# Expert outputs of three quads of four: a scatter by matmul, or indirect DMAs that add rows into sums in DRAM

## The chip, the cores and the metric

The kernel runs on one core of a Trainium2 chip. The metric is the device time of one execution in microseconds (us), as the median of several runs. Everything is float32.

## The reference, cut to what is computed

Two blocks follow each other. The first (two layers of attention, a state-space mixer and cross attention) is untouched by the change. The second has two layers of its own; each ends in a mixture of experts in which the experts choose their tokens:

```python
def _expert_choice_ffn(h, w_router, w_gate, w_up, w_down):
    cap = EC_CAPACITY_FACTOR * t // N_EXPERTS          # 64 of 512 tokens; 32 of 256 context tokens
    aff = softmax(h @ w_router)                        # tokens x 16 experts
    vals, idx = lax.top_k(aff.transpose(0, 2, 1), cap) # every expert picks cap tokens
    xg = h[idx]                                        # 16 x cap x 1024
    hid = silu(xg @ w_gate[e]) * (xg @ w_up[e])        # 1024 -> 512
    out = (hid @ w_down[e]) * vals[..., None]          # 512 -> 1024
    return zeros((t, d)).at[idx.reshape(-1)].add(out.reshape(-1, d))
```

Layer 0 does this for the 512 tokens of the sequence and, apart from them, for 256 context tokens; layer 1 (the last) for the 512 tokens alone. The result, times a modulation vector, is added to `x`.

## The kernel before

One Python program writes each engine's instruction list by hand; engines meet at semaphores. Activations lie feature-major in SBUF: `x` and `h` hold 8 tiles of 128 features by 512 tokens (and 256 context tokens). Matrices are not kept: all weights come from DRAM in the order of their use as one stream of units of 512 KB (128 partitions by 1024 floats). SyncE (SP) issues them (L350) into slots: a ring of 8 (`ring`), and in the expert phase also up to 6 tiles of `y_sb` and, in layer 1, 2 of `work` and 4 of `h_sb`. A slot is refilled when TensorE has turned to the next unit (`w_turn`); the planner `place_units` (L167) lays down which unit goes where. The slots in `y_sb` drop out as the quads' outputs come to need them, so for the last quad of layer 0 there are 10 slots and then 8, for that of layer 1 16 and then 14.

The second block's expert phase (`experts`, L683 for TensorE, L1061 for ScalarE, L1460 for VectorE, L1537 on for GpSimd):

- The router's logits give `aff`; `choose` (L1412) finds the 64 (32) best tokens of each expert and each token's rank among them. The normed tokens are turned token-major, and GpSimd stores them to the DRAM tensor `tokens` (L1560).
- The 16 experts go in four quads. For quad q, `one_hots` (L1442) makes matrices of tokens by slots: 4 blocks of 128 tokens by 4 experts x 64 slots, and for the context 2 blocks by 4 x 32 slots. `slot_tokens` (L734) multiplies them with the column of token numbers; VectorE casts the result to `slot_tok` (L1466), and GpSimd gathers the chosen rows with two indirect DMAs of 128 rows of 4 KB (three with the context; L1567). TensorE turns the rows (`turn_rows`, L745), after a wait for all gathers of the quad.
- Passes over the weights follow in this order: gate 0, then for each quad q: up q, gate q+1, down q (two halves). A pass of 16 units has two matmuls of 64 slots by 512 columns per unit, which run side by side in pairs, and in layer 0 two of 32 context slots, side by side in fours.
- `weigh` (L1451) multiplies the one-hots with the experts' `aff`; `transpose_one_hots` (L758) turns them, 8 transposes (10 with the context), and ScalarE copies them out (`spread_out`, L1102) to `spread`: slots by 512 tokens. The expert outputs stay slot-major in `out_e` (8 tiles of 128 slots by 1024) and `out_c` (4 such tiles, layer 0).
- The scatter is a matmul: for each of 8 feature tiles, `out_e` times `spread`. In layer 0 all of it stands at the end (L866 to L873): per feature tile 8 matmuls of 512 columns and 4 of 256. In layer 1 `scatter(q)` (L768) has two matmuls of 512 columns per feature tile for one quad; the steps of quads 0 to 2 are laid between the weight rounds of the next quad's passes (L805), those of quad 3 at the end. VectorE adds each result, times the modulation, to `x` (L1207 in layer 0, L1480 in layer 1), and in layer 1 SP stores the result (L354).

The helper `mm` is L1595: all matmuls but the transposes carry that line. A float32 matmul is two MATMUL records in the trace, a transpose one.

Of the kernel before, what the change touches and what calls it, by code (L numbers as in the profile page):

```python
# [12 lines left out]
P = 128  # L13
# [21 lines left out]
N_CONST = C_TOKEN + ALL // P  # L35
# [16 lines left out]
def build(nc, names, out):  # L52
# [4 lines left out]
    with ctx:  # L57
# [22 lines left out]
        slot_tok = ctx.enter_context(nc.sbuf_tensor("slot_tok", [P, 4], mybir.dt.uint32))  # L80
# [22 lines left out]
        rows_in = sem("rows_in")  # L103
# [13 lines left out]
        weighted_ready = sem("weighted_ready")  # L117
        quarters_ready = sem("quarters_ready")
        one_hot_read = sem("one_hot_read")
# [412 lines left out]
        def rows_until(both, q):  # L532

            return 3 * q if both else 3 * N_QUADS + 2 * q

# [22 lines left out]
        def slot_groups(both):  # L558
# [3 lines left out]
        spread = ([prob[:, n * T:(n + 1) * T] for n in range(3)] + [flat(10496 + n * T, T) for n in range(3)]  # L562
                  + [flat(n * T, T) for n in range(2)])
        spread_c = [levels_sb[:, n * CTX:(n + 1) * CTX] for n in range(3)] + [flat(2 * T, CTX)]

        def pe_second(pe, me, claim, freed, all_read, mm, weights, project, project_tokens, quarter_squares, add_quarters, attention, unit):
# [116 lines left out]
            def experts(both):  # L683
# [50 lines left out]
                def slot_tokens():  # L734
# [3 lines left out]
                    for n in range(2 + both):  # L738
                        for j in range(4 if n < 2 else 2):
                            of = one_hot[:, j, n * P:(n + 1) * P] if n < 2 else one_hot_c[:, j, :]  # L740
                            ins = mm(banks[6][:, n:n + 1], of, cst(C_TOKEN + j + (0 if n < 2 else 4), 1), j == 0,
                                     j == (3 if n < 2 else 1))
                    ins.then_inc(full_for_dve, 1)

                def turn_rows():  # L745

                    at["rows"] = at.get("rows", 0) + 1
                    pe.wait_ge(rows_in, 16 * rows_until(both, at["rows"]))
                    for n in range(2 * (2 + both)):
                        b = 6 + n % 2  # L750
                        claim(b, "act")
# [6 lines left out]
                def transpose_one_hots():  # L758

                    pe.wait_ge(weighted_ready, me.nth(weighted_ready))  # L760
# [6 lines left out]

                def scatter(q, written):  # L768

                    for f in range(KT):  # L770
                        b = 2 + 3 * (f % 2)
                        if f == 0:
                            pe.wait_ge(freed_by_act, written)
                        claim(b, "dve")
                        for m in (2 * q, 2 * q + 1):
                            ins = mm(banks[b][:, :], out_e[:, m, f * P:(f + 1) * P], spread[m], m == 2 * q, m == 2 * q + 1)
                        ins.then_inc(full_for_dve, 1)
                        yield

                def expert_pass(what, operand, rounds, reader, between=None):  # L780
# [3 lines left out]
                    for r in range(rounds):  # L784
# [20 lines left out]
                        next(at["scatter"], None)  # L805
# [24 lines left out]
                at = {"scatter": iter(())}  # L830
# [3 lines left out]
                expert_pass(("gate", 0), expert_input(0), 4, "act", lambda r: transpose_one_hots() if r == 2 else None)  # L834
                for q in range(N_QUADS):
# [23 lines left out]
                    if not both:  # L859
                        at["scatter"] = scatter(q, freed["act"])  # L860
                if not both:
                    for _ in at["scatter"]:
                        pass
                    return
                all_read("act")
                for f in range(KT):  # L866
                    fs = slice(f * P, (f + 1) * P)
                    for s, (o, sp_, n) in enumerate(((out_e, spread, 8), (out_c, spread_c, 4))):
                        b = 2 * (f % 2) + s
                        claim(b, "dve")  # L870
                        for m in range(n):
                            ins = mm(banks[b][:, 0:(T, CTX)[s]], o[:, m, fs], sp_[m], m == 0, m == n - 1)
# [74 lines left out]
        def act_second(act, me, A, bank_full, evacuate, squares, quarters, deviations, logs, attention):  # L947
# [113 lines left out]
            def experts(both):  # L1061
# [40 lines left out]
                def spread_out(q):  # L1102
                    for n in range(2):
                        evacuate(spread[2 * q + n], banks[6 + n][:, :])
                    if both:
                        evacuate(spread_c[q], banks[6][:, 0:CTX])
                    me.notify(one_hot_read)
# [8 lines left out]
                spread_out(0)  # L1116
# [1415 lines left out]
```

## Time and profile before

| | us |
|---|---|
| median of 3 runs | 3738.31 |
| lowest, highest | 3735.09, 3741.30 |
| the profiled execution's own time | 3735.97 |
| its span (first to last instruction) | 3734.2 |
| TensorE busy in the span | 3488.9 (93%) |
| mean granted TensorE clock | 0.968 |

The expert phase of layer 0 takes the span from about 2440 to 2849 us, that of layer 1 from about 3435 to the end. A span row gives busy time per engine, but a TensorE that is 93% busy over the whole says little on one stage: the stretches and the chain have to be asked stage by stage. A DMA share of 1.0 or more means that all 16 DMA engines always had a packet.

### The profile page before, as it was taken

How to read it: one execution, taken by the hardware profiler on the slowest of the kernel's cores; microseconds unless marked ns; L12 is line 12 of the kernel's file. 1: busy time of each engine (PE TensorE's matmuls, PEld its weight loads, DVE VectorE, ACT ScalarE, POOL GpSimd, SP SyncE). 2: the span in 40 equal slices, each digit the busy share in tenths (PEclk: the TensorE clock that was granted, in tenths of full speed). 3: DMA queues.
4: the chain of work that ended last, by engine and by line, in shares of the span. 5: the costliest groups of instructions: out<-in, count | busy, mean ns of one | idle time of the engine just before them, and what ended most of it. 6: DMA issues, size and time to landing. Idle time of an engine off the chain costs nothing.

```text
span 3734.2 us, 44667 instructions
## 1 busy us (share of the span) xinstructions
PE 3488.9 (93%) x18694; PEld 1959.9 (52%) x18694; DVE 1182.8 (32%) x2505; ACT 911.1 (24%) x1715; POOL 167.8 (4%) x192
## 2 busy tenths in 40 slices
PE   8999999999999989998999988979999999887899
PEld 4455454754465454754755766533334656663333
DVE  2322551022322451022343487120002334673011
ACT  1344130111344130113233321121112224211110
POOL 0000000000000000000000242010000000320000
PEclk9999999999999999999999999989999999799899
DMA  4111172312111172312101001169862110013897
GB/s 149 62 52 46 51 294 77 115 46 67 57 52 45 57 286 75 118 43 92 40 23 45 1 2 41 45 236 355 337 220 92 40 40 29 1 41 141 318 409 314
DMA packets 117414, 425.24 MB, mean 114 GB/s; under 512 B 12768, under 2 KB 14944, under 8 KB 116832
## 3 DMA queue, kind: packets, MB, share of 16 engines
q1 hardware_dynamic: 112896, 406.66, 29.6%
q0 software_dynamic: 4320, 15.73, 1.1%
q8 instruction: 150, 2.46, 0.3%
q14 instruction: 48, 0.39, 0.0%
HBM read 415.00 MB, written 7.34 MB: 113 GB/s over the span
## 4 chain that ended last, share of the span: by engine, by line
PE 85%; DVE 8%; DMA 3%; ACT 2%; issue 2%; POOL 0%; DVEq 0%; SPq 0%; ACTq 0%; POOLq 0%
PE bank L1595 82%; DMA ring<-in_stream 2%; PE bank L1710 1%; PE bank L754 1%; DMA work<-tokens,slot_tok 1%; DMA h_sb<-in_stream 0%; DVE work L1363 0%; DVE h_sb L2270 0%; ACT work L1957 0%; DVE work L2113 0%; DVE work L2115 0%; DVE levels L1363 0%; DVE work L1433 0%; DMA work<-in_stream 0%; DVE small L1432 0%
## 5 line engine op out<-in xcount | busy, mean ns | idle before, releaser
L1595 PE MATMUL bank<-h_sb,ring 128*128 128x512 f32 (+2 forms) x3200 | 1249.4, 547 | 25.5 <-ACT h_sb L972 8.2
L1595 PEld LDWEIGHTS bank<-h_sb,ring 128*128 128x128 f32 (+1 forms) x3200 | 592.5, 190 | 570.2 <-issue 529.7
L1595 PE MATMUL bank<-y_sb,ring 128*128 128x512 f32 (+1 forms) x1152 | 474.1, 573 | 9.7 <-DVEq L205 9.7
L1595 PEld LDWEIGHTS bank<-y_sb,ring 128*128 128x128 f32 x1152 | 219.1, 191 | 259.8 <-issue 245.1
L1917 ACT ACTIVATE work<-bank 128x512 f32<-128x512 f32 (+1 forms) x262 | 133.0, 519 | 797.1 <-PE bank L1595 645.3
L1595 PE MATMUL bank<-work 128*64 128x128 f32 (+7 forms) x2016 | 291.8, 346 | 26.6 <-DVE small L2120 12.2
L1595 PE MATMUL bank<-ring,h_sb 128*128 128x128 f32 (+2 forms) x2144 | 284.8, 311 | 1.4 <-ACT work L1087 0.7
L1595 PEld LDWEIGHTS bank<-ring,h_sb 128*128 128x128 f32 (+2 forms) x2144 | 232.2, 185 | 42.3 <-issue 39.2
L1595 PEld LDWEIGHTS bank<-work 64*128 64x128 f32 (+2 forms) x2016 | 183.6, 170 | 116.2 <-issue 78.8
L1595 PE MATMUL bank<-ring,work 128*64 128x512 f32 (+1 forms) x800 | 210.0, 596 | 0.7 <-DMA ring<-in_stream 0.6
L1595 PE MATMUL bank<-y_sb,work 128*64 128x128 f32 (+2 forms) x920 | 169.2, 430 | 1.4 <-DMA ring<-in_stream 0.7
L1595 PE MATMUL bank<-work,y_sb 128*128 128x512 f32 (+1 forms) x496 | 138.1, 437 | 14.0 <-DVE ring L1335 3.6
L1928 ACT ACTIVATE h_sb<-x_sb 128x1024 f32<-128x1024 f32 (+1 forms) x56 | 48.0, 896 | 407.0 <-DVEq L205 400.8
L1917 ACT ACTIVATE y_sb<-bank 128x512 f32<-128x512 f32 (+1 forms) x163 | 86.8, 555 | 185.0 <-PE bank L1595 172.9
L2125 DVE TENSOR_REDUCE small<-bank 128x1 f32<-128x256 f32 (+3 forms) x96 | 41.7, 466 | 261.5 <-PE bank L1595 261.3
L1548 POOL MEMSET work<- 128x1024 f32 x4 | 3.7, 949 | 2548.4 <-DVEq L205 2548.4
L1595 PEld LDWEIGHTS bank<-ring,work 128*64 128x64 f32 (+1 forms) x800 | 57.4, 129 | 97.4 <-issue 97.3
L1595 PEld LDWEIGHTS bank<-work,y_sb 128*128 128x128 f32 (+1 forms) x496 | 59.5, 170 | 86.4 <-issue 65.2
L1957 ACT ACTIVATE work<-work,small 128x256 f32<-128x256 f32 (+3 forms) x124 | 73.1, 590 | 128.5 <-DVEq L205 128.5
L1595 PE MATMUL bank<-ring 64*128 64x128 f32 x840 | 85.9, 321 | 19.4 <-DVE work L1363 15.9
L1710 PEld LDWEIGHTS bank<-const,work 128*128 128x128 f32 x576 | 69.5, 141 | 57.0 <-issue 40.4
L1595 PEld LDWEIGHTS bank<-y_sb,work 128*64 128x64 f32 (+1 forms) x920 | 61.5, 132 | 69.3 <-issue 64.5
(293 smaller groups left out, 3575.0 us busy)
## 6 DMA issues: line engine op xcount, KB each, us to landing
ring<-in_stream SPq DMA_DIRECT2D x578, 512.0 KB, 4.6
y_sb<-in_stream SPq DMA_DIRECT2D x110, 512.0 KB
h_sb<-in_stream SPq DMA_DIRECT2D x40, 512.0 KB, 14.8
work<-in_stream SPq DMA_DIRECT2D x20, 512.0 KB, 15.3
work<-in_bias SPq DMA_DIRECT2D x2, 2688.0 KB, 9.4
tokens<-work POOLq DMA_DIRECT2D x10, 512.0 KB, 4.5
x_sb<-in_xT SPq DMA_DIRECT2D x4, 512.0 KB, 6.4
out<-x_sb SPq DMA_DIRECT2D x8, 256.0 KB, 2.0
```

Of the source, the lines that this page charges most:

```text
L754: ins = nc.tensor.transpose(banks[b][:, k * P:(k + 1) * P], picked[:, n // 2, ks], ident)
L1548: ins = V.memset(level_sums[d][n], 0.0)
L1595: return nc.tensor.matmul(o, a, b, start=first, stop=last, skip_group_check=True)
L1710: ins = nc.tensor.transpose(banks[b][:, j * P:(j + 1) * P], scores_in(i - 1, s)[:, kb * P:(kb + 1) * P], ident)
L1917: me.link(A(o, i, func, **kw), freed_by_act, wait=False)
L1928: me.link(A(dst[:, k:k + 2, :], src[:, k:k + 2, :], ACT.Square), squares_ready, wait=False)
L1957: me.link(A(at, banks[s][:, 0:u["nk"]] if raw else at, ACT.Exp, bias=nmax[:, j:j + 1], scale=1.0 if raw else -1.0, accum_out=rsum[:, j:j + ...
L2125: me.link(V.reduce_max(m, banks[s][:, 0:nk], AX.X, negate=True), max_ready, wait=False)
```

## The change

1. In both layers the outputs of quads 0 to 2 no longer go through a matmul. GpSimd adds each group of 128 slot rows (512 KB) by an indirect DMA with `compute_op=add` into `sums[l]` in DRAM, at the rows of their tokens (`put_tok`). Two experts of one group may pick the same token, so the two halves of a group add into different copies of the sums (two copies for the tokens, four for the context), and GpSimd waits between DMAs that touch the same copy. That makes 9 such DMAs in layer 0 and 6 in layer 1.
2. After quad 2 GpSimd reads the sums back into `h_tok`: copy 0 plainly, each other copy with an accumulating DMA behind it. Layer 0: six DMAs in four steps (2 x 2 MB and 4 x 1 MB); layer 1: two of 2 MB, one after the other.
3. At the end of each layer TensorE waits for the sums, and per feature tile has quad 3's two matmuls of 512 columns (and one of 256 for the context) and turns the sums by matmuls with the identity into the same bank: 4 of 128 columns (and 2 for the context).
4. `scatter`, `weigh` and their waits go; only quad 3's one-hots are transposed. The slot's weight goes into the product of gate and up (`slot_val`); it comes out of `slot_tokens`, whose moving operand grows from one column to five.
5. The gathers get a semaphore for each group, and `turn_rows` waits for one group at a time.
6. At the start GpSimd fills `sums` with zeros: 24 DMAs of 512 KB after TensorE's twelfth unit. ScalarE waits for them ahead of the first block's second attention.

```diff
                 def slot_tokens():
...
-                            ins = mm(banks[6][:, n:n + 1], of, cst(C_TOKEN + j + (0 if n < 2 else 4), 1), j == 0,
+                            ins = mm(banks[6][:, 5 * n:5 * n + 5], of, token_val[:, j + (0 if n < 2 else 4), :], j == 0,
                                      j == (3 if n < 2 else 1))
                 def turn_rows():
...
-                    pe.wait_ge(rows_in, 16 * rows_until(both, at["rows"]))
                     for n in range(2 * (2 + both)):
                         b = 6 + n % 2
+                        if n % 2 == 0:
+                            pe.wait_ge(rows_in[n // 2], 16 * (at["rows"] + (0 if both or n == 4 else N_QUADS)))
...
-                expert_pass(("gate", 0), expert_input(0), 4, "act", lambda r: transpose_one_hots() if r == 2 else None)
+                expert_pass(("gate", 0), expert_input(0), 4, "act")
...
-                        if r == 2:
+                        if r == 2 and q + 2 == N_QUADS:
                             transpose_one_hots()
...
-                    if not both:
-                        at["scatter"] = scatter(q, freed["act"])
-                if not both:
-                    for _ in at["scatter"]:
-                        pass
-                    return
                 all_read("act")
+                pe.wait_ge(sums_in, 16 * sum(steps_of_sums(n) for n in range(DEPTH - both)))
                 for f in range(KT):
                     fs = slice(f * P, (f + 1) * P)
-                    for s, (o, sp_, n) in enumerate(((out_e, spread, 8), (out_c, spread_c, 4))):
+                    for s in range(1 + both):
                         b = 2 * (f % 2) + s
                         claim(b, "dve")
-                        for m in range(n):
-                            ins = mm(banks[b][:, 0:(T, CTX)[s]], o[:, m, fs], sp_[m], m == 0, m == n - 1)
+                        if s:
+                            mm(banks[b][:, 0:CTX], out_c[:, N_QUADS - 1, fs], spread_c, True, False)
+                        else:
+                            for m in range(2):
+                                mm(banks[b][:, :], out_e[:, 2 * N_QUADS - 2 + m, fs], spread[m], m == 0, False)
+                        for j in range(2 if s else 4):
+                            ins = mm(banks[b][:, j * P:(j + 1) * P], sums_tok[:, 4 * s + j, fs], ident, False,
+                                     j == (1 if s else 3))
                         ins.then_inc(full_for_dve, 1)
```

VectorE, per quad (`chosen_tokens` replaces the cast, `weigh` goes):

```diff
+                me.link(V.tensor_copy(as_rows(slot_tok[:, cols]), found[:, :, 0:1]))
+                me.notify(slots_ready)
+                me.link(V.tensor_tensor(as_rows(put_tok[:, cols]), found[:, :, 0:1], as_rows(cst(C_PUT, n)), ALU.add))
+                for e in range(QUAD):
+                    rows, g = slice(CAP * (e % 2), CAP * (e % 2) + CAP), e // 2
+                    me.link(V.tensor_copy(slot_val[rows, 3 * q + g:3 * q + g + 1], found[rows, g, 1 + e:2 + e]))
...
-                        me.link(V.tensor_tensor(hidden[m], hidden[m], banks[first_bank["up", q] + m][:, :], ALU.mult),
+                        me.link(V.scalar_tensor_tensor(out=hidden[m], in0=hidden[m], scalar=slot_val[:, 3 * q + m:3 * q + m + 1],
+                                                       in1=banks[first_bank["up", q] + m][:, :], op0=ALU.mult, op1=ALU.mult),
                                 freed_by_dve)
```

GpSimd (`rows_scaled` comes from ScalarE when both halves of down q have been copied out):

```diff
+            pool.wait_ge(w_turn, 12)
+            for l in range(DEPTH):
+                for n in range(sums[l].shape[0] // P):
+                    V.dma_start(sums[l][n * P:(n + 1) * P, :], zeros).then_inc(zeros_stored, 16)
...
+                def add_rows(q, n):
+                    o = out_c[:, q, :] if n == 2 else out_e[:, 2 * q + n, :]
+                    V.indirect_dma_start(sums[l], bass.IndirectOffsetOnAxis(put_tok[:, 3 * q + n:3 * q + n + 1], 0), o, None,
+                                         compute_op=ALU.add).then_inc(rows_added, 16)
...
+                for q in range(N_QUADS - 1):
+                    pool.wait_ge(rows_scaled, (N_QUADS - 1) * l + q + 1)
+                    add_rows(q, 0)
+                    if both:
+                        add_rows(q, 2)
+                    if q + 2 < N_QUADS:
+                        fetch_rows(q + 2)
+                    rows_there()
+                    add_rows(q, 1)
+                    if q + 2 < N_QUADS:
+                        rows_there()
+                pool.wait_ge(gather_read, N_QUADS * (l + 1))
+                if both:
+                    read_sums(True, 0)
+                    rows_there()
+                    sums_there()
+                    read_sums(False, 0)
+                    read_sums(True, 1)
+                    sums_there()
+                    read_sums(False, 1)
+                    read_sums(True, 2)
+                    sums_there()
+                    read_sums(True, 3)
+                else:
+                    rows_there()
+                    read_sums(False, 0)
+                    sums_there()
+                    read_sums(False, 1)
+                sums_there()
```

`read_sums(of_ctx, copy)` is one DMA, with `accum_op=add` where copy is not 0. `rows_there()` and `sums_there()` wait for all issued so far.

## Rows read from the trace of the kernel before

**Rows 1.** The page: span, busy time, DMA share (tenths) in 40 slices of the span.

```profile
span 3734.2 us, 44667 instructions
...
PE 3488.9 (93%) x18694; PEld 1959.9 (52%) x18694; DVE 1182.8 (32%) x2505; ACT 911.1 (24%) x1715; POOL 167.8 (4%) x192
...
DMA  4111172312111172312101001169862110013897
```

**Rows 2.** Stretches of chosen length: window, length, busy (instructions) per engine, PEclk, DMA share, GB/s.

```profile
2479.70:2727.00 247.30, 243.93 (x1484) 81.23 (x1472) 16.30 (x24) 39.68 (x75) 8.42 (x9) 1.00 0.90 343
2727.00:2779.00 52.00, 47.39 (x270) 13.52 (x268) 2.06 (x3) 5.82 (x10) 0.00 (x0) 0.97 0.74 271
2779.00:2849.00 70.00, 69.01 (x192) 36.40 (x192) 9.94 (x17) 1.45 (x3) 0.00 (x0) 1.00 0.00 0
3474.70:3707.30 232.60, 226.64 (x986) 82.85 (x984) 29.84 (x39) 29.62 (x51) 5.61 (x6) 1.00 1.02 404
3707.30:3734.20 26.90, 23.58 (x68) 9.07 (x64) 7.51 (x10) 1.19 (x2) 0.00 (x0) 1.00 0.22 84
```

**Rows 3.** Stretches of 20 and 2 us, layer 1's experts, around the weights' last landing.

```profile
3490.00:3510.00 20.00, 19.15 (x102) 8.25 (x103) 1.93 (x4) 2.48 (x5) 1.87 (x2) 1.00 1.03 409
...
3534.00:3536.00 2.00, 1.38 (x8) 0.50 (x8) 0.00 (x0) 0.00 (x0) 0.00 (x0) 1.00 1.05 416
3706.00:3708.00 2.00, 2.00 (x11) 0.77 (x12) 0.75 (x1) 0.00 (x0) 0.00 (x0) 1.00 0.67 262
```

**Rows 4.** The chain that ended last, 2700 to 2860: start, us, what.

```profile
2726.91 6.50 DMA ring<-in_stream
...
2759.12 6.52 DMA ring<-in_stream
...
2779.09 69.03 PE bank L1595 x192
```

**Rows 5.** Timeline in the final scatter of layer 0: start, us, engine, line, operation.

```profile
2839.35 7.03 PE L1595 MATMUL bank<-work,y_sb 128*128 128x512 f32 x16
...
2846.22 1.46 PE L1595 MATMUL bank<-levels,h_sb 128*128 128x256 f32 x6
```

**Rows 6.** Groups by shape over the whole span: busy us, mean ns.

```profile
L1595 PE MATMUL bank<-ring,h_sb 128*128 128x128 f32 x1920 | 220.3, 276 | 0.0
```

**Rows 7.** The chain in layer 0: last gather landing; one-hots turned and copied.

```profile
2467.82 5.12 DMA work<-tokens,slot_tok
...
2548.36 0.60 PE bank L765 x4
...
2548.99 0.61 ACT work L1917
...
2549.64 0.44 PE bank L765 x2
```

**Rows 8.** DMA issues of the page: queue, count, KB each, us to landing.

```profile
tokens<-work POOLq DMA_DIRECT2D x10, 512.0 KB, 4.5
```

**Rows 9.** The chain in layer 1: the gathers of quads 0 and 1 landing.

```profile
3463.16 5.02 DMA work<-tokens,slot_tok
...
3493.27 9.24 DMA work<-tokens,slot_tok
```

**Rows 10.** Stretches of 20 us in which the zeros will be stored, and a cold one.

```profile
100.00:120.00 20.00, 20.00 (x63) 9.04 (x62) 5.29 (x22) 10.71 (x29) 0.00 (x0) 1.00 0.24 79
...
2460.00:2480.00 20.00, 10.03 (x56) 7.96 (x58) 1.81 (x3) 3.70 (x8) 3.27 (x3) 0.59 0.24 79
```

**Rows 11.** Timeline of the last 20 us.

```profile
3715.16 15.72 PE L1595 MATMUL bank<-work,y_sb 128*128 128x512 f32 x36
...
3719.81 12.28 SPq L354 DMA_DIRECT2D out<-x_sb  x8
...
3730.92 0.75 DVE L1480 SCALAR_TENSOR_TENSOR x_sb<-bank,modv_sb,x_sb 128x512 f32<-128x512 f32 x1 [0.97 <-PE bank L1595]
```

More of the change, by code:

```diff
@@ L79, in build @@
         acc_o = sb("acc_o", ALL)
-        slot_tok = ctx.enter_context(nc.sbuf_tensor("slot_tok", [P, 4], mybir.dt.uint32))
+        slot_tok = ctx.enter_context(nc.sbuf_tensor("slot_tok", [P, 12], mybir.dt.uint32))
+        put_tok = ctx.enter_context(nc.sbuf_tensor("put_tok", [P, 12], mybir.dt.uint32))
+        slot_val = ctx.enter_context(nc.sbuf_tensor("slot_val", [P, 12], f32))
+        sums = [nc.dram_tensor(f"sums{l}", (2 * SEQ + (4 * CTX if l < DEPTH - 1 else 0), D_MODEL), f32).ap()
+                for l in range(DEPTH)]
         tokens = nc.dram_tensor("tokens", (ALL, D_MODEL), f32).ap()
@@ L102, in build @@
         slots_ready = sem("slots_ready")
-        rows_in = sem("rows_in")
+        rows_in = [sem(f"rows_in{n}") for n in range(3)]
         w_turn = sem("w_turn")
@@ L560, in slot_groups, with steps_of_sums @@
             return ([(2, CAP_CTX, range(4))] if both else []) + [(0, CAP, (0, 1)), (1, CAP, (2, 3))]
-        spread = ([prob[:, n * T:(n + 1) * T] for n in range(3)] + [flat(10496 + n * T, T) for n in range(3)]
-                  + [flat(n * T, T) for n in range(2)])
-        spread_c = [levels_sb[:, n * CTX:(n + 1) * CTX] for n in range(3)] + [flat(2 * T, CTX)]
+        spread = [prob[:, n * T:(n + 1) * T] for n in range(2)]
+        spread_c = levels_sb[:, 0:CTX]
+        token_val = small[:, 220:250].rearrange("p (j n) -> p j n", j=6)
+        sums_tok = h_tok
+        ZERO_TILES = sum(v.shape[0] // P for v in sums)
+        def steps_of_sums(l):
+            return 6 if need_ctx(l) else 2
         def pe_second(pe, me, claim, freed, all_read, mm, weights, project, project_tokens, quarter_squares, add_quarters, attention, unit):
@@ L1486, in experts @@
-                earlier = iter(())
                 for q in range(N_QUADS):
                     if q + 1 < N_QUADS:
-                        chosen_tokens()
-                    for _ in range(3):
-                        next(earlier, None)
+                        chosen_tokens(q + 1, both)
+                    if q + 2 < N_QUADS:
+                        one_hots(q + 2, both)
                     for m, _, _ in slot_groups(both):
@@ L1561, in _, with fetch_rows @@
                 pool.wait_ge(tokens_stored, 16 * (6 * l + n_tok))
-                for q in range(N_QUADS):
+                both, at = need_ctx(l), {"added": (N_QUADS - 1) * 3 * l, "in": steps_of_sums(0) * l}
+                def fetch_rows(q):
                     pool.wait_ge(slots_ready, N_QUADS * l + q + 1)
@@ new lines, in add_rows, with rows_there, read_sums @@
+                def add_rows(q, n):
+                    o = out_c[:, q, :] if n == 2 else out_e[:, 2 * q + n, :]
+                    V.indirect_dma_start(sums[l], bass.IndirectOffsetOnAxis(put_tok[:, 3 * q + n:3 * q + n + 1], 0), o, None,
+                                         compute_op=ALU.add).then_inc(rows_added, 16)
+                    at["added"] += 1
+                def rows_there():
+                    pool.wait_ge(rows_added, 16 * at["added"])
+                def read_sums(of_ctx, copy):
+                    first, n, to = (2 * SEQ, CTX, slice(4, 6)) if of_ctx else (0, SEQ, slice(0, 4))
+                    v = sums[l][first + copy * n:first + copy * n + n, :].rearrange("(j p) f -> p j f", p=P)
+                    if copy:
+                        ins = V.dma_start(sums_tok[:, to, :], v, accum_op=ALU.add)
+                    else:
+                        ins = V.dma_start(sums_tok[:, to, :], v)
+                    ins.then_inc(sums_in, 16)
+                    at["in"] += 1
```

117 lines of the change are left out of this document (52 added, 65 removed).

## The prediction

> **What bounds the kernel now.** The page comes first [rows 1]: TensorE is busy for 93% of the span, so the kernel as a whole is TensorE's. But the DMA digits are 8 and 9 in two places, which are the two expert phases. So the second view is the stretches [rows 2]. In layer 1, from 3474.7 to 3707.3, the DMA share is 1.02 at 404 GB/s while TensorE counts as busy for 97%. Both look full. The finer stretches part them [rows 3]: 409 GB/s at a share of 1.03 from the first refills on; in the 2 us from 3534 TensorE has 0.6 us of holes and the DMA engines none; at 3706 to 3708 the rate falls to 262, so the last weights land at about 3707.3. The weight stream of layer 1 is DMA-bound from its first refill to its last landing, and TensorE merely has about as much to do. In layer 0 it is the other way round: up to 2727 the share is 0.90, then 0.74, and during the final scatter, 2779 to 2849, it is 0.00 [rows 2]. The chain shows that scatter as one piece of 69.03 us, with nothing beside it; it also shows two waits for a weight unit, 6.5 us from issue to landing each, in the last quad [rows 4], where few slots are left: there the DMA already sits close to TensorE.
>
> **Prices.** A unit of 512 KB (0.524 MB) takes 0.524/409 = 1.28 us of all 16 engines. A MATMUL record of 512 columns takes 6.87/16 = 0.43 us (from 2839.35 to 2846.22), so a matmul 0.86 and one of 256 columns 0.43 [rows 5]. A matmul of 128 columns takes 2 x 220.3/1920 = 0.23 us [rows 6].
>
> **Layer 0, TensorE.** The final scatter becomes, per feature tile, 2 x 0.86 + 0.43 + 6 x 0.23 = 3.53 us, times 8 = 28.2 in place of 69.0: 40.8 us less, and nothing covers it, so it is all on the path. Three of four turned one-hots go: 0.60 + 0.61 + 0.44 and the issue between [rows 7], 1.7 us each, 5.2 in all. The first gather is awaited group by group: the third lands where it did [rows 7], but only its own 8 transposes are then left of 24: about 3 us. Against it stand two small VectorE copies ahead of the first one-hots, 0.4 us, taking a cast's 0.16 us each. The eight or so further small copies per quad lie beside a pass of 20 us and cost nothing; they have only the `hidden` product queued behind them. If that cover went they would cost 2 us a quad. Five moving columns for one: nothing, such records are as long as their weight load. So down 2 ends at 2727 - 8 = 2719, if the DMA lets it: the stretch before 2727 moved 343 GB/s [rows 2], which leaves 247.3 x (1 - 343/409) = 40 us of DMA time to spare, and the six adds of quads 0 and 1 take 15 of it at the price below.
>
> **What an add costs.** No row shows an accumulating DMA. From below it is a copy: 1.28 us per 512 KB. From above, 4.5 us, the whole time from issue to landing of a store of 512 KB into DRAM [rows 8], as if nothing overlapped. I take 2.56: old rows and new rows have both to be read, which is two copies' worth of reading, and that is nearest to the lower row. The Trainium skill ("Collectives: The Full Stack", the section on why ReduceScatter is half of AllGather) says that an add passing through a DMA engine has two source reads and so runs at half a copy's rate. No row here shows that; by the copy's price the sum below would be -14 us, by the page's rule it is the one that I give.
>
> **Layer 0, the new chain.** After down 2 GpSimd has five steps in a row, each waiting for the one before: two adds; one add with a plain read of 1 MB; 2 MB plain with 1 MB accumulated; 3 MB accumulated; 1 MB accumulated. A step's fixed part comes from a gather of 512 KB with idle engines: 5.02 us [rows 9] less 1.28 = 3.7, and 1.2 more where a second is issued behind it. While weights stream, both queues share the engines: the same gather took 9.24 us then [rows 9], which fits packets served in turn (one of the weights' for each of GpSimd's). So the steps take, with 3.84 us per accumulated 512 KB and 2.56 per plain one: 7.7 + 4.9 = 12.6; 9.0 + 4.9 = 13.9; 17.9 + 4.9 = 22.8; together 49.3, in which the weights have moved 11 units beside them and 11 in the gaps. Between 2727 and 2779 they need 271 GB/s x 52 us = 14.1 MB = 27 units [rows 2], so 5 are left: 15.4 + 6.4 + 4.9 = 26.7; and the last step 5.1 + 3.7 = 8.8. The sums are in 85 us after down 2, at 2804. TensorE would be ready 52 us after it, at 2771, and stands for 33 us: this is the new wait, and only GpSimd's chain is late. The quad's last units come a little later than before, inside that wait. A stretch after such a wait was granted a clock of 0.59 [rows 10], so 2 us more. The phase ends at 2804 + 28.2 + 2 = 2834 for 2848.1: **-14 us**. The Trainium skill ("DMA: Bandwidth & Descriptors", the section on one DMA's anatomy) fits a fixed part of about 2.0 us where the gather's row gives 3.7; by it five steps would be some 9 us shorter and the sum +6. The row is taken, as this kernel's own.
>
> **Layer 1.** Here TensorE's relief (3 quads x 8 x 4 records of 0.43 = 41 us, and transposes) is worth nothing: the weights land no earlier. What counts is what is added to a full DMA queue: 6 adds x 2.56 = 15.4, 2 MB plain 5.1, 2 MB accumulated 10.2: **+30.7 us** on the last landing. The first gather is awaited by group and the refills start some 1.5 us earlier: -1.5. The chain of four steps takes 7.5 + 7.5 + 14 + 20 = 49 us, and the 32 units left after down 2 take 41 + 20.5 = 61, so the sums are in first and TensorE does not wait for them. From last landing to end: before, 26.9 us [rows 2], with quad 2's scatter still interleaved, down 3 ending at 3715.2 [rows 11]. After: the last four matmuls, in pairs, 1.7; issue and the output copy 0.9; 8 x (2 x 0.86 + 4 x 0.23) = 21.1; VectorE 0.75 and the last store 2.5 [rows 11]: 27.0. TensorE's new 7.4 us of identity matmuls and the 8 us by which it no longer trails cancel. Layer 1: **+29 us**.
>
> **Zeros.** 24 stores, 31 us of DMA time, begin near 100 us, where the share is 0.24 [rows 10] and 8 slots of about 7 us each are filled ahead; ScalarE's wait comes some 100 us later. Nothing; if the cover failed, up to 10 us.
>
> **Sum.** 3735.97 (this execution, 2.3 us under the median) - 14 + 29 = 3751; against the median of 3738.3 that is 3753.
>
> **Rivals.** *A, an add costs a copy.* Then layer 0's steps are 10.0, 12.6, 20.3, 19.0 and 6.3 = 68 us, the scatter starts at 2787 and the phase ends at 2817: -31. Layer 1 gets 7.7 + 5.1 + 5.1 - 1.5 = +16.5. Total -14: 3724, faster. For it: a gather costs what a copy does though it is indirect [rows 9]. Against: twice the reading. Its place is the engines' read side, and it decides where an add takes under 1.9 us per 512 KB (each 0.1 us of that price moves the whole by 2.3): below that the kernel is not slower.
> *B, the chain hides.* GpSimd's packets are served first or steps overlap better, so layer 0 keeps all of its 49 us and only layer 1 pays: -49 + 29 = -20, 3718; faster. Against it: 41 us of new DMA time and 35 of weights after down 2 do not fit into 52.
> *C, adds are dearer,* near the store's 4.5 us: layer 0's chain takes 107 us (+8), layer 1 gets 27 + 5 + 18 = +50: 3796.
> *D, layer 1 isn't DMA-bound,* its 1.02 an artefact of TensorE's pace: then 41 us come off there and the 7 of identity matmuls go on, and the kernel is at 3738 - 14 - 34 = 3690. The full rate during TensorE's holes speaks against it [rows 3].
>
> **How the numbers follow.** The forecast, 3753, has 0.47; A 0.26; B 0.07; C 0.16; D 0.04. The forecast's own range is 3738 to 3775. The range to hold 8 in 10 takes in A's centre and most of C's lower part: 3720 to 3788. About 0.2% (7.5 us) is what a measurement can tell from no change. Slower: forecast without its lowest part 0.42, C 0.16, so 0.58; within: 0.05 of the forecast and 0.09 of A's upper part, 0.14; faster: 0.28.
>
> **What would show it.** Right: layer 1's phase at 409 GB/s to about 3735 with holes on TensorE all along it; in layer 0 a TensorE wait of 25 to 40 us for a DMA into `work` ahead of the last scatter, which is 28 us long; adds of 8 us from issue to landing beside weights. Wrong: that wait under 10 us (B), adds landing as fast as gathers (A), weights in layer 1 ending with DMA shares under 1, or a stall in the first 300 us.

## The result, and the profile after the change

The changed kernel takes 3763.37 us (median; 3759.36 to 3767.24), the kernel before on the same chip 3737.7: a ratio of 1.0065 (95% interval 1.0048 to 1.0082). It is slower, by about 26 us. Run again later beside another run of the kernel before (e12 below), it was 1.005 (1.0034 to 1.0066).

The page of the changed kernel, against [rows 1]:

```profile
span 3759.3 us, 44451 instructions
...
PE 3438.1 (91%) x18560; PEld 1939.5 (52%) x18560; DVE 1165.5 (31%) x2535; ACT 904.3 (24%) x1700; POOL 217.2 (6%) x240
...
DMA  4511172312111172312001001269982110014997
...
q0 software_dynamic: 13136, 48.76, 4.4%
...
sums<-y_sb,put_tok POOLq DMA_INDIRECT x12, 9.2
work<-sums POOLq DMA_DIRECT2D x4, 2048.0 KB, 15.2
```

TensorE has 51 us less to do and the kernel is longer. The DMA digits are higher in both expert phases. The same stretches as in [rows 2]:

```profile
2479.70:2727.00 247.30, 241.21 (x1446) 78.61 (x1448) 14.91 (x45) 34.56 (x65) 19.73 (x15) 0.99 0.96 352
2727.00:2779.00 52.00, 41.59 (x218) 11.89 (x214) 2.24 (x3) 4.17 (x8) 7.59 (x6) 0.90 1.02 344
2779.00:2849.00 70.00, 49.87 (x236) 26.64 (x236) 10.23 (x18) 9.54 (x14) 3.65 (x3) 0.83 0.50 128
3474.70:3707.30 232.60, 185.76 (x822) 65.35 (x818) 11.62 (x30) 24.22 (x42) 17.55 (x13) 0.95 1.03 398
3707.30:3734.20 26.90, 14.57 (x48) 4.17 (x48) 0.00 (x0) 1.79 (x3) 1.35 (x1) 0.81 0.86 262
```

Two readings. In layer 1 (fourth row) the DMA share stays at 1.03 and TensorE's busy time falls from 226.6 to 185.8 us: its relief has turned into idle time, and the weights still flow at the old end of the stretch (fifth row, share 0.86 for 0.22). In layer 0 the stretch from 2727 to 2779 has gone from a share of 0.74 to 1.02: in the last quad there the DMA engines are now full too.

**Where the 25 us lie.** One execution was profiled per kernel, and the first 2330 us, in which only the zeros are new, vary by up to 15 us between kernels. So phases are compared: from the start of the long TensorE piece of the chain (90 us, at 2332.2 before, "the mark") to the first piece after layer 0's experts (6.5 us); from there to layer 1's first gather; from there to the end.

| us | before the mark | layer 0's experts | between | layer 1's experts | span |
|---|---|---|---|---|---|
| before | 2332.2 | 517.9 | 611.4 | 272.8 | 3734.2 |
| after | 2335.1 | 509.2 | 614.0 | 301.1 | 3759.3 |
| difference | +2.8 | -8.7 | +2.6 | +28.3 | +25.1 |

The forecast had -14 and +29. Layer 0 was -10.8 to -12.0 in three other kernels with the same layer 0 (e3, e5, e12), so -8.7 is the low end of some 3 us of spread. In e12, the same kernel again, layer 1 was +31.0 and the stretch between the layers 619.8 us. A difference of 2 or 3 us between two phases is therefore not a finding.

The chain that ended last in layer 0, against [rows 4]:

```profile
2716.83 7.27 DMA ring<-in_stream
...
2734.87 10.95 DMA ring<-in_stream
...
2752.46 8.86 DMA ring<-in_stream
...
2772.47 9.88 DMA ring<-in_stream
...
2783.84 10.08 DMA ring<-in_stream
...
2794.05 6.86 PE bank L1648 x32
...
2801.55 9.59 issue
2811.14 31.14 PE bank L1648 x144
```

The 69.03 us of scatter are 31.1 now. The forecast's new wait is the row "issue", a wait for which the profile names no releaser: TensorE stands until the last read of the sums, issued at 2802.5 (below), is in. That is 9.6 us, not 33. Ahead of it stands what the forecast had put inside that wait: units that take 7 to 11 us to land, where [rows 4] had 6.5 twice, so that the last quad itself ends at 2801 and not at 2771. The scatter then takes 31.1 us, 2.9 more than in e4 below; its granted clock was 0.90.

GpSimd's timeline there (start, us, engine, line, operation, and in brackets the idle time before it):

```profile
2731.24 1.57 POOL L1568 DMA_INDIRECT sums<-y_sb,put_tok  x1 [65.48 <-ACTq L213]
2733.11 1.56 POOL L1568 DMA_INDIRECT sums<-h_sb,put_tok  x1 [0.30 <-issue]
2745.70 1.56 POOL L1568 DMA_INDIRECT sums<-y_sb,put_tok  x1 [11.03 <-DMA sums<-h_sb,put_tok]
...
2760.92 0.82 POOL L1583 DMA_DIRECT2D work<-sums  x1 [12.83 <-DMA work<-sums]
...
2781.37 2.48 POOL L1581 DMA_DIRECT2D work<-sums  x2 [18.38 <-DMA work<-sums]
2802.53 1.16 POOL L1581 DMA_DIRECT2D work<-sums  x1 [18.67 <-DMA work<-sums]
```

Its five steps took 14.5, 15.2, 20.5, 21.2 and 8.6 us, together 79.9 (forecast: 12.6, 13.9, 22.8, 26.7, 8.8; 85). The chain took about as long as forecast; what it is hidden behind did not.

For the end of layer 1, first its chain, then TensorE's waits from 3470 to 3765 (for what: us, times, longest):

```profile
3702.53 26.41 DMA ring<-in_stream
...
3729.08 5.12 PE bank L1648 x16
...
3734.87 21.16 PE bank L1648 x96
```

```profile
PE bank L1648 <- DMA ring<-in_stream: 29.4, 22, 6.3
PE bank L1648 <- DMA h_sb<-in_stream: 12.6, 12, 3.0
PE bank L1648 <- DMA y_sb<-in_stream: 8.0, 10, 3.5
PE bank L1648 <- DMA work<-in_stream: 7.4, 7, 2.7
```

Some 57 us of waits for weight units, in slots of every kind, and no wait for the sums in the chain: the scatter starts as soon as the last quad is copied out. From the last unit's landing at 3729.0 to the end lie 30.3 us, where the last row of [rows 2] is 26.9 long.

### The profile page after: what moved, and what is told of

It reads as the page before. It is cut to its first block, busy times and chain, and to the rows that moved or that the text cites. A ratio compares the mean times of both kernels' runs of the same rounds, so it can differ in the third digit from the quotient of the medians.

```text
span 3759.3 us, 44451 instructions
## 1 busy us (share of the span) xinstructions
PE 3438.1 (91%) x18560; PEld 1939.5 (52%) x18560; DVE 1165.5 (31%) x2535; ACT 904.3 (24%) x1700; POOL 217.2 (6%) x240
## 4 chain that ended last, share of the span: by engine, by line
PE 79%; DMA 9%; DVE 7%; ACT 2%; issue 2%; POOL 0%; SPq 0%; DVEq 0%; ACTq 0%; POOLq 0%
PE bank L1648 77%; DMA ring<-in_stream 6%; PE bank L1763 1%; DMA y_sb<-in_stream 1%; DMA h_sb<-in_stream 1%; DVE work L1364 0%; ACT work L2010 0%; PE bank L766 0%; DMA work<-in_stream 0%; DVE work L2168 0%; DVE levels L1364 0%; DVE work L2170 0%; DVE h_sb L2325 0%; DVE work L1434 0%; DVE small L1433 0%
## 5 line engine op out<-in xcount | busy, mean ns | idle before, releaser
L1648 PE MATMUL bank<-work 128*64 128x128 f32 (+7 forms) x2016 | 295.9, 349 | 30.2 <-DVE small L2175 12.1
L1648 PE MATMUL bank<-ring,work 128*64 128x512 f32 (+1 forms) x800 | 217.7, 618 | 26.0 <-DMA ring<-in_stream 23.2
L1648 PE MATMUL bank<-work,const 128*128 128x256 f32 (+3 forms) x208 | 94.7, 602 | 3.2 <-ACTq L213 3.2
L1763 PE MATMUL bank<-const,work 128*128 128x128 f32 x576 | 84.4, 276 | 11.0 <-ACT y_sb L1970 11.0
## 6 DMA issues: line engine op xcount, KB each, us to landing
work<-sums POOLq DMA_DIRECT2D x4, 2048.0 KB, 15.2
```

What stands on the lines that cost most here:

```text
L1648: return nc.tensor.matmul(o, a, b, start=first, stop=last, skip_group_check=True)
L1763: ins = nc.tensor.transpose(banks[b][:, j * P:(j + 1) * P], scores_in(i - 1, s)[:, kb * P:(kb + 1) * P], ident)
```

## The experiments

e1 to e4 are the changed kernel with one part taken out. e5 to e8 are mixtures, in which a list says for each layer how many quads go by DRAM; the others keep the scatter by matmul. e9 and e10 are parts of e5.

### e1: the adds as copies

```diff
                     V.indirect_dma_start(sums[l], bass.IndirectOffsetOnAxis(put_tok[:, 3 * q + n:3 * q + n + 1], 0), o, None,
-                                         compute_op=ALU.add).then_inc(rows_added, 16)
+                                         ).then_inc(rows_added, 16)
```

> The changed kernel, but the 15 indirect DMAs into the sums store their rows without adding them (the sums then hold only the last rows stored). Bytes, waits and order stay. Theory (an added 512 KB takes about 2.56 us of the engines, a stored one 1.28): layer 1 gets shorter by 6 x 1.28 = 7.7 us, layer 0's last chain by some 4 to 8 us, together 12 to 16 us under the changed kernel, near 3749. Rival A (an add costs a copy): no change, 3763.

Measured: 3748.95 us, 1.0033 of before (1.0018 to 1.0048), as expected. Layer 0's experts took 499.1 us (-10.1 against the changed kernel), layer 1's 295.0 (-6.1). The last pair in layer 1, in the changed kernel and then in e1:

```profile
3674.34 1.57 POOL L1568 DMA_INDIRECT sums<-y_sb,put_tok  x1 [57.79 <-ACTq L213]
3683.65 1.57 POOL L1568 DMA_INDIRECT sums<-y_sb,put_tok  x1 [7.73 <-DMA sums<-y_sb,put_tok]
```

```profile
3666.80 0.98 POOL L1568 DMA_INDIRECT sums<-y_sb,put_tok  x1 [57.53 <-ACTq L213]
3674.39 0.96 POOL L1568 DMA_INDIRECT sums<-y_sb,put_tok  x1 [6.60 <-DMA sums<-y_sb,put_tok]
```

An add follows its forerunner by 9.3 us, a copy by 7.6, and an add also holds GpSimd 0.6 us longer. In a phase that is DMA-bound nearly from end to end, six adds cost 6.1 us more than six copies: **1.0 us per 512 KB on top of a copy's 1.28**, so 2.3 in all. Against layer 1 of e12, which is the changed kernel again and 2.7 us longer there, it is 1.5 and 2.8. Both are nearer to the 2.56 taken than to either bound, and above the 1.9 at which rival A begins.

### e2: the accumulating reads as plain ones

```diff
-                    if copy:
-                        ins = V.dma_start(sums_tok[:, to, :], v, accum_op=ALU.add)
-                    else:
-                        ins = V.dma_start(sums_tok[:, to, :], v)
+                    ins = V.dma_start(sums_tok[:, to, :], v)
```

> The changed kernel, but every copy of the sums is read back plainly over the one before, not accumulated. Theory (accumulating costs twice a copy's engine time): layer 1 shorter by 2 MB x 1.28 per 512 KB = 5.1 us, layer 0's chain by up to 10 x 1.28 = 12.8 us, most of it in TensorE's wait: 15 to 18 us under the changed kernel, near 3747. Rival A: no change, 3763.

Measured: 3740.64 us, 1.0011 (0.9995 to 1.0027): 6 us under what was expected. Layer 0 took 494.6 us (-14.5), layer 1 295.1 (-6.0). Layer 1 has 2 MB of accumulated reading, so that is **1.5 us per 512 KB on top of the copy**, 2.8 in all (2.2 and 3.5 against e12). With one profiled execution each, this does not show that an accumulating read is dearer than an accumulating write: by the last landing of a weight in layer 1, counted from the first gather, e1 gains 8.6 us and e2 only 2.8, which gives the opposite order. The two experiments together take 12 of layer 1's 28 us away. The other 16 are left for the plain transport, which 14 units at 1.28 us put at 18; no run has both parts out at once.

### e3 and e4: no adds and reads, in layer 1 and in both

```diff
             def add_rows(q, n):
+                if not both:
+                    return
...
             def read_sums(of_ctx, copy):
+                if not both:
+                    return
```

e4 returns always, and its TensorE and GpSimd wait for no sums.

> The changed kernel without layer 1's six adds and two reads (layer 1 then turns whatever lies in the room of the sums). TensorE's work stays as changed. Theory (layer 1 is bound by its weight stream, the new traffic adds to it one for one, and TensorE's relief is worth nothing): layer 1 comes back to the length that it had before, so the kernel is 28 to 32 us under the changed one, near 3733. Rival D (TensorE sets layer 1's pace): 40 us or more below that, since 41 us of scatter are gone: under 3700.

> As the run without layer 1's traffic, and layer 0's nine adds and six reads gone too: only the change on TensorE, VectorE and ScalarE is left. Theory: layer 0 now keeps the 41 us of its final scatter and some 8 us of turned one-hots and earlier gathers, layer 1 is unchanged: 3738 - 49 = 3689, with TensorE going straight from down 3 into the final scatter. If layer 0 is nearer to its weight stream than the stretch's share of 0.90 tells, the 8 us are missing: 3697.

Measured: e3 3732.26 us, 0.9986 (0.9974 to 0.9998), layer 1's experts 274.0 us where the kernel before has 272.8. TensorE has 41 us less matmul there and nothing comes of it. Rival D is out. e3 also gives a price without e1 and e2. All of layer 1's new traffic together costs 27.1 us (29.8 in e12), and the last landing moves by 24.0 (26.3). Less 5.1 for the plain read, this leaves 1.9 to 2.5 us for each of the ten accumulated 512 KB. The price of an accumulated 512 KB is thus known as some 1.9 to 2.8 us, and no closer.

e4: 3696.81 us, 0.9902 (0.9877 to 0.9926), the higher of the two figures it was given. Layer 0's experts took 474.3 us, -43.5 against before. Its chain:

```profile
2709.89 5.92 DMA ring<-in_stream
...
2720.99 6.30 DMA ring<-in_stream
...
2732.46 7.15 DMA ring<-in_stream
...
2754.84 6.61 DMA ring<-in_stream
...
2773.25 28.19 PE bank L1651 x144
```

The scatter is 28.19 us (forecast 28.2). But the last quad ends 444.2 us after the mark, where the kernel before has 446.9: of the 8 us of earlier shift only 2.7 came, without any traffic of sums at all. The four waits for units do not explain it: TensorE waits 4.7 us for weights in this phase, where it waited 3.0 before. What is missing lies behind `slot_tokens`, whose 20 records are as short as before. The matmuls after them are not. The kernel before, then e4 (the timeline, and 2 us of the stretch with its granted clock of 0.61, mostly the lower of the clock's two levels, where the kernel before has 1.00):

```profile
2577.20 2.39 PE L1595 MATMUL bank<-const,work 128*128 128x1 f32 x20
2579.52 6.05 PE L1595 MATMUL bank<-y_sb,work 128*32 128x512 f32 x33
```

```profile
2569.31 2.40 PE L1651 MATMUL bank<-small,work 128*128 128x5 f32 x20
2571.64 7.70 PE L1651 MATMUL bank<-y_sb,work 128*32 128x512 f32 x33
2574.00:2576.00 2.00, 2.00 (x8) 0.44 (x6) 1.62 (x3) 0.00 (x0) 1.69 (x2) 0.61 0.98 358
```

The same 33 records take 1.65 us longer. Such a dip comes at all three quads in e4, at two in the changed kernel, and at none in the kernel before. Three times 1.65 is 5.0 us, and with the 2.7 that came it makes 7.7 of the 8. Each dip eats what one turned one-hot had saved (the period of a quad is 75.06 us before, 73.42 without a dip and 75.06 with one). Whether the five moving columns cause the dips stays open: e1 and e8 have the same columns and no dip, and e1's layer 0 is 3.3 us shorter by that alone, so that 6.8 of its 10.1 us are left for the adds.

### e5: only layer 0 by DRAM

```diff
-                        if r == 2 and q + 2 == N_QUADS:
+                        if r == 2 and turned_quad(l, q + 1):
                             transpose_one_hots()
...
+                    if not both:
+                        at["scatter"] = scatter(q, freed["act"])
```

`turned_quad(l, q)` is `q >= VIA[l]` with `VIA = (3, 0)`; `scatter` is the one that the change removed.

> Layer 0 as in the changed kernel (quads 0 to 2 through sums in DRAM), layer 1 with the scatter by matmul between the weight rounds as before, no traffic of its own. Theory (layer 1's 27 to 28 us are the price of its traffic, layer 0's part is a gain of about 9 us): 3738 - 9 = 3729. Rival (what is off in the changed kernel is spread over both layers, or lies in the common parts such as slot weights and zeros): above 3738.

Measured: 3724.66 us, 0.9954 (0.9936 to 0.9971), 4 us under what was expected. Layer 0's experts took 507.1 us (-10.8), as in the whole change, so layer 0 of this change is a gain of its own. Layer 1's took 268.5, where the kernel before has 272.8; in the kernels with the same layer 1 (e5 to e11) it varies from 268.3 to 272.2.

### e6: two quads by DRAM instead of three

`VIA = (2, 0)`, so 6 adds and the same 8 MB of reads, which start one quad earlier; the final scatter has quad 2 in it too.

> As the run before it, but in layer 0 only quads 0 and 1 go through DRAM, so that nothing of the chain lies behind down 2; quad 2's scatter by matmul costs TensorE 8 x (2 x 0.86 + 0.43) = 17 us at the end. Theory (behind down 2 the chain of adds and reads costs about 30 us, 20 of them because it takes the engines from the weights): that wait goes, 17 us come in, and the expert phase of layer 0 is 12 to 16 us shorter than before: 3722 to 3726. Rival (the reads are dear wherever they lie, since the phase has no 48 us of DMA time to spare): at or above the run with three quads, 3729 or more.

Measured: 3742.21 us, 1.0004 (0.9994 to 1.0015): a miss by 16 us, on the rival's side. The wait for the sums has gone, but the chain has this instead:

```profile
2694.48 16.87 DMA y_sb<-in_stream
...
2712.54 21.86 DMA ring<-in_stream
...
2808.51 45.37 PE bank L1702 x192
```

The reads now all lie among the last weights, and single ones of these take 17 and 22 us to land. The last quad ends 472.3 us after the mark, later than in any other kernel here. In the changed kernel about a third of the reads' DMA time (12 of 36 us, worked out as for the table below) comes after the last weight and delays none; in e6 nothing of it does. This is what the expectation for e6 lacked.

### e7 and e8: only the token rows by DRAM

The context (a third of the slots, but half of the bytes that are read, because it has four copies of 1 MB) keeps its matmul: `steps_of_sums` is 2, only groups 0 and 1 are added, and TensorE has four matmuls of 256 columns per feature tile as before. e7 takes three quads by DRAM, e8 two.

```diff
                         add_rows(q, 0)
-                        add_rows(q, 2)
...
-                if both:
-                    read_sums(True, 0)
-                    rows_there()
-                    sums_there()
-                    read_sums(False, 0)
-                    read_sums(True, 1)
-                    sums_there()
-                    read_sums(False, 1)
-                    read_sums(True, 2)
-                    sums_there()
-                    read_sums(True, 3)
-                sums_there()
+                rows_there()
+                read_sums(False, 0)
+                sums_there()
+                read_sums(False, 1)
+                sums_there()
```

> Layer 0 sends only the rows of the 512 tokens of quads 0 to 2 through DRAM (6 adds, 2 reads of 2 MB); the context rows, whose sums have four copies and cost 18 us of DMA time to read back, are scattered by matmul as before: 8 x (3 x 0.43 - 2 x 0.23) = 6.6 us of TensorE more than in the changed kernel. Layer 1 as before the change. Theory (31 us of new DMA time fit into the phase's 40 us of room; the chain behind down 2 is add, add, read, read, some 55 us beside TensorE's 52): layer 0's phase is 25 to 33 us shorter than before: 3705 to 3713. Rival (the wait for the sums is set by the number of steps, not by bytes): no more than 10 us better than the run with all rows of three quads, 3719 or more.

> As the run with token rows only, but of quads 0 and 1 alone: 4 adds, and reads that have time until down 3 ends; quad 2's tokens cost TensorE 8 x 1.72 = 13.8 us. Theory: if the chain behind down 2 is hidden with three quads, this one is 10 to 14 us slower than that; if the chain still costs more than 14 us there, this one is faster. Expected near 3718.

Measured: e7 3715.02 us, 0.9937 (0.9915 to 0.996); e8 3726.17, 0.9964 (0.9948 to 0.998). e7 is faster than both kernels of this case. It lies 2 us above its expected range and 4 below its rival's bound. e8 lies 8 us above its own expected 3718, and 11 above e7, inside the 10 to 14 that were expected between the two: its last quad ends 6 us earlier (the table below; 3 of them are two clock dips less), and its final scatter is 14 us longer. In e7 no wait for the sums is left:

```profile
2773.59 8.99 DMA ring<-in_stream
...
2782.72 7.08 PE bank L1695 x32
2789.82 0.61 ACT y_sb L2017
...
2790.47 34.98 PE bank L1695 x160
```

### e9 and e10: adds alone, reads alone

What was still open is which of the two delays layer 0's last quad. Both are e5 with one kind left out.

> Layer 1 is as before the change. In layer 0 the nine adds stay and the six reads of the sums are left out, so that TensorE turns stale rows and waits only for the adds (output not the reference's). Account: what delays layer 0 is DMA time that is taken from the weights between 2576 us and the last weight; the kernel without any traffic ended its last quad 444 us after the mark near 2332 us, the one with adds and reads in layer 0 alone 463 us. The adds are 21 to 23 us of DMA time and the slots hide 15 to 22, so they alone should cost 0 to 6 us: from the mark to the next phase's first piece 474 to 480 us, and about 3692 to 3699 us in all (e5_only_layer0 had 507 us and 3724.7). Rival: the adds, which wait for each other and come where units are tight, are the dear part: 490 us or more, 3708 or more.

> As e5_only_layer0, but the nine adds are left out and the six reads stay (the output is not the reference's). GpSimd can begin the reads at about 2732 us, some 15 us earlier, and its four steps took 65 us, so the sums are in at 2792 to 2797 us. The reads take their time from the last 30 units, where no slot is filled ahead: the last quad should end at 2775 to 2785 us, TensorE then waits 10 to 18 us for the sums, and from the mark to the next phase it takes 488 to 496 us: 3706 to 3714 us in all. Rival (the adds are the dear part): the last quad ends at 2773 us and the sums are the only wait, with reads that run faster for want of adds: under 486 us, under 3704.

Measured: e9 3706.78 us, 0.9899 (0.9876 to 0.9922), 8 us over its range. Part of that lies where nothing was edited: its profiled execution reached the mark 7 us later than e5's. The phase took 479.3 us, inside the 474 to 480. e10: 3720.88 us, 0.9951 (0.9932 to 0.9969), also over its range; from the mark to the end of the scatter 491.8 us, which with the 2 us that follow in the other kernels is 494, inside the 488 to 496. The split inside it was not as expected: the last quad ended at 2797.4 for the expected 2775 to 2785, and no wait for the sums was left. The last long rows of the chain, of e9 and then of e10:

```profile
2781.82 4.94 DMA ring<-in_stream
...
2786.89 5.56 PE bank L1703 x32
...
2793.12 28.19 PE bank L1703 x144
```

```profile
2743.30 14.03 DMA ring<-in_stream
...
2765.28 18.66 DMA ring<-in_stream
...
2797.39 28.19 PE bank L1703 x144
```

The nine adds alone delay the last quad by 4.9 us, the reads alone by 19.4. The reads are the dearer part of layer 0. The two runs do not part it cleanly, though: without the adds, e10's reads begin 392 us after the mark and the changed kernel's 412, so more of them fall before the last weight. This fits with the reads alone (463.6) being as late as reads and adds together in e5 (463.3), and with e1, which makes only the adds cheaper and still gains.

### e11 and e12: e7 and the changed kernel again, on one chip

> The kernel of e7_tokens_only again, in more rounds and beside the changed kernel on the same chip. It gave 3715.0 us, 0.9937 of the kernel before, in four runs; the same is expected here: 3711 to 3719, 0.993 to 0.995.

> The changed kernel itself, beside e11 on the same chip: 3763 us and 1.0065 of the kernel before as in its first runs, so that e11 is 45 to 52 us faster than it. If the first figure was of its chip and not of the kernel, it lies elsewhere by more than 4 us.

Measured beside a kernel before of 3740.81 us: e11 3718.55 us, 0.9946 (0.993 to 0.9961); e12 3760.09 us, 1.005 (1.0034 to 1.0066). In e12 layer 0's experts took 505.9 us and layer 1's 303.8. e11, with the token rows of layer 0 alone, beats the changed kernel by 42 us, a little less than the 45 expected, and the kernel before by 22.

### Layer 0 in one table

How late the last quad ends against e4, with the DMA time that was added ahead of the last weight, an estimate at e1's and e2's 2.3 us per added 512 KB, 1.28 per plain and 2.8 per accumulated one. Of the changed kernel's 56 us the last 1 MB and some 40% of the 3 MB step came after the last weight, of e10's 36 the last 1 MB. e7 and e8 also turn the context's one-hots of each quad, e6 and e8 those of quad 2, and the number of clock dips differs (last column).

| | DMA time added, us | last quad after the mark | later than e4 | then waits for sums | dips |
|---|---|---|---|---|---|
| e4, none | 0 | 444.2 | 0 | 0 | 3 |
| e9, adds | 21 | 449.1 | 4.9 | - | 2 |
| e8, tokens, two quads | 25 | 453.4 | 9.2 | 0 | 0 |
| e7, tokens, three quads | 30 | 459.4 | 15.2 | 0 | 2 |
| e10, reads | 30 | 463.6 | 19.4 | 0 | 2 |
| after | 44 | 466.5 | 22.3 | 9.6 | 2 |
| the same layer 0 in e3, e5, e12 | 44 | 462.8 to 464.8 | 18.6 to 20.6 | 9.1 to 11.6 | 2 or 3 |
| e6, two quads | 50 | 472.3 | 28.1 | 0 | 1 |

Most of the order is the same in both columns: the first 15 us or so seem free, and from 21 to 50 us of added DMA time the delay grows by 23 us. But it is not one us for one everywhere. From e10 to the changed kernel 14 us are added, and the delay changes by -1 to +3. TensorE's own saving in this layer is 43.5 us (e4), and the changed kernel gives 22 back in late weights, 10 in the wait for the sums and 3 in the longer scatter.

## Why the prediction came out right

- **The bound.** Layer 1 is DMA-bound and TensorE's relief is worth nothing there: shown by e3 (274.0 us against 272.8), and by the 57 us of waits for units in the changed kernel.
- **The price of an add.** 2.56 was taken; e1 shows 2.3, e2 2.8 for an accumulating read, and e3 1.9 to 2.5 for both together. The size is about right, and the runs place it no better. By the rule of the Trainium skill ("Collectives: The Full Stack", why ReduceScatter is half of AllGather), with this case's 1.28 for a copy, both would be 2.56; the runs' figures lie on either side of it. The reason, two reads for one write, is not proved by this, only its size.
- **Layer 1, +29.** Measured +28.3, and the nearness is in part luck, because two errors cancel. Counted from the first gather, the last landing moved by 24.9 us against the kernel before, not by 30.7 - 1.5 = 29.2. The accumulating read was in 0.7 us after the last weight, so nearly all of the traffic counts here, and it was cheaper than forecast. From the last landing to the end it took 30.3 us for the 27.0 forecast (27.2 in e3): 16 records of the last quad were left and took 5.1 us at a granted clock of 0.72, where e3 had 8 left that took 2.0. The early refill (-1.5) did not show: e3's last landing is 0.9 us later than that of the kernel before.
- **Layer 0, -14.** Measured -8.7, and -10.8 to -12.0 in its repetitions. The total is near, but two of its steps failed. First, "down 2 ends at 2727 - 8 = 2719": GpSimd's third group of adds starts at 2731.24, which by the mark is 9.4 us later than that. e4 shows that only 2.7 of the 8 us were there, and that clock dips behind `slot_tokens` took 5.0. The prediction had put that place at nothing ("Five moving columns for one: nothing"); the records themselves are as short as it said. The changed kernel lost 3.3 by two dips, and had 2.6 of waits for weights ahead of that point, where the kernel before has none. The spare 40 us had been worked out from the rate (343 of 409 GB/s). The share in the same row, 0.90, says 25, and a mean over 247 us does not show the stretches in which it was full. Second, "the quad's last units come a little later than before, inside that wait": the last quad ended 20 us later after the mark than before (28 later than forecast), and so the wait for the sums was 9.6 us and not 33. The end hardly moved by it, because it hung on GpSimd's chain: 9.4 us later in its start, 4.9 shorter (79.9 for 85), and a scatter 0.9 longer than the 30.2 forecast, together the 5 us between -14 and -8.7. That a wait forecast at 33 us and measured at 9.6 leaves the sum nearly right is luck.
- **The chain's fixed part.** The last step, with idle engines, took 8.6 us for the 8.8 worked out with 3.7 from the gather's row. By the 2.0 of the Trainium skill ("DMA: Bandwidth & Descriptors", one DMA's anatomy) it would have been 7.1. With e2's 2.8 us for each accumulated 512 KB in place of 2.56 the fixed part is 3.0, still above the 2.0.
- **Zeros, 0.** The stretches from 100 to 160 show shares of 0.70, 1.02 and 0.37, and TensorE waits for no weights there. The mark is 2.8 us later. TensorE is 5.1 us behind already at the end of its first 32 records on weights (which take 17.05 us for 13.97), before the zeros are issued at 106.
- **The other 10 us.** The forecast was 3753 and the kernel takes 3763. By the table of phases 5 us of this are layer 0's, 5 lie in the stretches for which it had nothing (2.8 before the mark, 2.6 between the layers, both within their spread), and layer 1 gives 1 back.
- **The rivals.** A fell by the time of both layers (it had -31 and +16.5) and by e1, in which copies are cheaper than adds. C fell by the price (1.9 to 2.8, below 4.5), D by e3. B, that layer 0 keeps its whole gain, is nearly what e4 (-43.5) and e9 (-38.6) have, but not beside the reads. By the prediction's own signs, a wait under 10 us was to speak for B, and one of 25 to 40 for the forecast. The wait was 9.6 and B was still wrong: the sign could not tell a chain that is early from a last quad that is late.

What stays open: whether an accumulating read costs more than an accumulating write, what brings the clock dips, and the 2.6 us between the layers, a stretch that in kernels with the same code there varies from 610 to 620.

## What to carry to other kernels

Work that is moved from TensorE to the DMA queues has to be priced in the phase where it lands: where the queues are full, nearly all of it goes on the end (24 to 30 us in layer 1), and the same edit was worth -9 to -12 us in one layer and +28 in the other. Move only the part with the best ratio of matmul saved to bytes moved (here the token rows, which have two copies and not four), and put bulk reads behind the last weight or where slots are filled ahead, not among the last units. Spare DMA time is better read from the share of short stretches than from a rate averaged over the phase. And a forecast wait at a meeting of two chains checks only their difference: look at the end of each chain by itself.

## What the runs showed that was not expected

An accumulating DMA costs GpSimd more as well: 1.57 us to issue for 0.98 of the same indirect DMA without the add (e1). Beside adds and reads of the sums, a DMA share of 1.02 goes with 344 GB/s (2727 to 2779), where the weights alone reach 409 at 1.03. The engines are as full; that what they read for the sum is not counted as moved is one reading, which no run tests. Starting the reads earlier (e6) cost more than starting them late: single units of weights then took 17 to 22 us to land.
